# The first mixer kind in another order: two-softmax heads first, then the scan, plain attention last

## The reference, cut to what matters

```python
h = rms_norm(x, attn_norm[l])
proj = h @ w_in[l]                      # 1024 x 3072, padded to 26 chunks of 128 columns
a_q, a_k, a_v, b_q, b_k, b_v, c_q, c_ff, c_fb, c_v, c_g = split_columns(proj)
# A: plain attention, 6 query heads on 2 key heads of width 64, normed and rotated (rope)
aq = rope(rms_norm(a_q)); ak = rope(rms_norm(a_k)); o_a = softmax(aq ak^T / 8) @ av
# B: 4 heads, each the difference of two softmaxes of width 48, value width 96
p = softmax(q1 k1^T * s + bias) - lam * softmax(q2 k2^T * s + bias)
o_b = rms_norm(p @ bv) * (1 - lam_init)
# C: gated linear scan, both directions, 4 heads of 64
f = lb + (1 - lb) * sigmoid(c_ff or c_fb); cq = silu(c_q)
o_c = rms_norm(scan_forward + scan_backward) * silu(c_g)
x = x + concat(o_a, o_b, o_c) @ w_out[l]
```

## Time and profile before

| | us |
|---|---|
| Profiled execution, its own time | 1835.33 |
| Its span on the core | 1833.6 |
| TensorE busy | 1673.1 (91%) |
| VectorE busy | 1273.2 (69%) |
| ScalarE busy | 988.9 (54%) |
| GpSimd busy | 531.1 (29%) |
| TensorE clock granted, mean | 0.948 of full |
| First mixer of this kind, first unit to first output unit | 17.00 to 191.77 |
| Second mixer of this kind | 405.95 to 573.94 |

### The profile page before, as it was taken

The page is one execution under the profiler, slowest core; times in us unless marked ns, Lnnn a source line. Parts: engine busy times, 40 slices in busy tenths (PEclk is TensorE's granted clock), DMA queues, the critical chain, the costliest instruction groups (busy, mean ns, idle before and its releaser), DMA issues. The chain is left out here.

```text
span 1833.6 us, 30207 instructions
## 1 busy us (share of the span) xinstructions
PE 1673.1 (91%) x10188; PEld 1448.8 (79%) x10188; DVE 1273.2 (69%) x2018; ACT 988.9 (54%) x1530; POOL 531.1 (29%) x511
## 2 busy tenths in 40 slices
PE   5896899999976999999999476999999999799999
PEld 5785799888856999888888335888888888568888
DVE  5675677756776777667757877777577765757763
ACT  5455466545563666466644344665376535446652
POOL 3040433310312334134410003443144411434430
PEclk9998899999997999999999658999999999789999
DMA  6330355654311456555654202556555654225563
GB/s 229 104 116 24 100 181 185 219 169 139 104 58 57 163 185 204 184 177 188 209 186 133 86 1 86 178 185 215 164 181 185 209 180 149 69 92 184 186 217 102
DMA packets 70793, 274.12 MB, mean 150 GB/s; under 512 B 7872, under 2 KB 9024, under 8 KB 70592
## 3 DMA queue, kind: packets, MB, share of 16 engines
q1 hardware_dynamic: 70272, 271.04, 45.9%
q0 software_dynamic: 448, 2.13, 0.3%
HBM read 272.09 MB, written 1.05 MB: 149 GB/s over the span
## 5 line engine op out<-in xcount | busy, mean ns | idle before, releaser
L761 DVE TENSOR_TENSOR wl<-raw,wh 128x1024 fp32r<-128x1024 f32 (+1 forms) x474 | 626.6, 1322 | 104.7 <-ACT wh L507 98.1
L507 ACT ACTIVATE wh<-raw 128x1024 fp32r<-128x1024 f32 (+1 forms) x474 | 529.2, 1118 | 211.9 <-PE gb L1170 125.2
L1166 PE MATMUL gb<-hx,wh 128*128 128x512 f32 x1540 | 554.0, 399 | 0.0
L1167 PE MATMUL gb<-hx,wl 128*128 128x256 f32 x1540 | 432.3, 281 | 0.0
L1166 PE MATMUL gb<-gux,wh 128*128 128x512 f32 x960 | 341.1, 394 | 0.0
L1166 PEld LDWEIGHTS gb<-hx,wh 128*128 128x128 f32 x1540 | 289.8, 188 | 60.7
L1153 PE MATMUL gb<-hx,wh 128*128 128x256 f32 x1008 | 299.2, 297 | 24.8 <-DVE wl L761 17.4
L1167 PEld LDWEIGHTS gb<-hx,wl 128*128 128x128 f32 x1540 | 291.0, 189 | 7.9
L1154 PE MATMUL gb<-hx,wh 128*128 128x256 f32 x1008 | 288.7, 286 | 0.0
L1155 PE MATMUL gb<-hx,wl 128*128 128x256 f32 x1008 | 288.2, 286 | 0.0
L1167 PE MATMUL gb<-gux,wl 128*128 128x256 f32 x960 | 268.1, 279 | 0.0
(11 more groups left out here) (213 smaller groups left out, 2140.7 us busy)
## 6 DMA issues: line engine op xcount, KB each, us to landing
raw<-in_wa SPq DMA_DIRECT2D x378, 512.0 KB, 3.5
raw<-in_wb SPq DMA_DIRECT2D x96, 704.0 KB, 4.1
x<-in_x SPq DMA_DIRECT2D x1, 1024.0 KB, 5.0
out_x<-x SPq DMA_DIRECT2D x8, 128.0 KB, 3.2
row<-in_row POOLq DMA_DIRECT2D x1, 836.0 KB, 10.6
tab<-in_bias SPq DMA_DIRECT2D x3, 256.0 KB, 4.6
con<-in_const POOLq DMA_DIRECT2D x1, 544.0 KB, 7.7
tab<-in_bias SPq DMA_DIRECT2D x1, 512.0 KB, 5.2
```

What stands on the lines that cost most here:

```text
L507: nc.scalar.activation(wh[:, slot, 0:nt * P], raw[:, slot, 0:nt * P], ACT.Copy).then_inc(s_hi, 1)
L761: nc.vector.tensor_tensor(wl[:, slot, 0:nt * P], raw[:, slot, 0:nt * P], wh[:, slot, 0:nt * P].bitcast(f32), ALU.subtract).then_inc(s_lo, 1)
L1166: nc.tensor.matmul(bank[:, :], a, both(k), start=start and k == 0, stop=False)
L1167: nc.tensor.matmul(bank[:, 0:SEQ], b, high(k), start=False, stop=False)
```

## The change

Chunks, heads and steps of `mix1` get a new order; head steps are entries of their own (`turnp`, `score`, `prob`, `attend`) in place of `attn`, and `out_norms` is split into `stats` (statistics) and `post` (scaling and on). For `even` and `odd`, `spread` writes each old `attn` entry out as the four new ones in the order the engines had.

```diff
-M1_AQ, M1_AK, M1_AV, M1_CQ, M1_CF, M1_CB, M1_CG, M1_CV, M1_BV, M1_B = 0, 3, 4, 5, 7, 9, 11, 13, 15, 18
-A_ORDER = [0, 3, 1, 4, 2, 5]
+M1_CQ, M1_CF, M1_CB, M1_CG, M1_BV, M1_CV, M1_AK, M1_AV = 4, 6, 8, 10, 12, 19, 22, 25
+M1_AQ = (23, 24, 21)
+M1_B = (0, 2, 15, 17)
+A_ORDER = [2, 5, 0, 3, 1, 4]
...
-        W = {"mix1": [(1, "sqr", 0), (2, "sum", 0), (2, "norm", 0), (3, "sqr", 1), (4, "sum", 1), (4, "norm", 1),
-                      (5, "rotate", 0), (5, "rope", 0), (6, "turn", 0), (7, "rotate", 1), (7, "rope", 1),
-                      (9, "attn", 0), (10, "attn", 1), (11, "attn", 2), (12, "attn", 3), (13, "attn", 4), (13, "gates", 0),
-                      (14, "attn", 5), (16, "level", 0), (17, "turn", 1), (17, "level", 1), (18, "turn", 2),
-                      (18, "level", 2), (19, "level", 3), (19, "turn", 3), (20, "level", 4), (20, "turn", 4), (20, "sqr", 2),
-                      (21, "level", 5), (21, "sum", 2), (21, "norm", 2), (22, "level", 6), (22, "sqr", 3), (23, "level", 7),
-                      (23, "sum", 3), (23, "attn", 6), (23, "norm", 3), (24, "level", 8), (24, "sqr", 4), (25, "sum", 4),
-                      (25, "norm", 4), (25, "attn", 7), (25, "sqr", 5), (26, "cout", 0), (26, "sum", 5), (26, "norm", 5)] +
-                     [(26, "attn", t) for t in range(8, 14)] + [(26, "post", 0)],
+        W = {"mix1": [(1, "sqr", 0), (2, "sum", 0), (2, "norm", 0), (3, "sqr", 1), (4, "score", 0), (4, "sum", 1), (4, "norm", 1),
+                      (6, "prob", 0), (6, "score", 1), (7, "turnp", 0), (8, "prob", 1), (9, "turnp", 1), (12, "gates", 0),
+                      (13, "turn", 0), (14, "turn", 1), (15, "turn", 2), (15, "level", 0), (16, "attend", 0), (16, "level", 1),
+                      (17, "sqr", 2), (17, "attend", 1), (17, "level", 2), (18, "sum", 2), (18, "norm", 2), (18, "level", 3),
+                      (19, "sqr", 3), (19, "level", 4), (19, "score", 2), (20, "sum", 3), (20, "norm", 3), (20, "prob", 2),
+                      (20, "level", 5), (21, "turnp", 2), (21, "turn", 3), (21, "level", 6), (21, "score", 3),
+                      (22, "attend", 2), (22, "prob", 3), (22, "level", 7), (23, "sqr", 4), (23, "turnp", 3), (23, "level", 8),
+                      (23, "sum", 4), (23, "norm", 4), (24, "attend", 3), (24, "cout", 0), (25, "sqr", 5), (25, "rotate", 0),
+                      (25, "sum", 5), (25, "rope", 0), (25, "stats", 0), (25, "norm", 5), (26, "score", 4), (26, "turn", 4),
+                      (26, "rotate", 1), (26, "rope", 1), (26, "score", 5), (26, "prob", 4), (26, "turnp", 4), (26, "score", 6),
+                      (26, "prob", 5), (26, "post", 0), (26, "turnp", 5), (26, "score", 7), (26, "prob", 6), (26, "attend", 4),
+                      (26, "turnp", 6), (26, "score", 8), (26, "prob", 7), (26, "attend", 5), (26, "turnp", 7), (26, "score", 9),
+                      (26, "prob", 8), (26, "attend", 6), (26, "turnp", 8), (26, "prob", 9), (26, "attend", 7),
+                      (26, "turnp", 9), (26, "attend", 8), (26, "attend", 9)],
...
-            return u % 4 if kind != "mix1" or u < 13 else u % 2
+            return u % 4 if kind != "mix1" or u < 12 else u % 2
...
             def rope(m, g):
-                yv, tmp = pair(yc(2 * g, 2)), pair(ptb[:, 0, :])
+                yv, tmp = pair(yc(M1_AQ[2] + 2 * g, 2)), tap[:, :, :]
-                nc.vector.tensor_tensor(tmp, pair(MISC[:, :]), both(C_SIN), ALU.mult)
+                nc.vector.tensor_tensor(tmp, pair(gb[3][:, :]), both(C_SIN), ALU.mult)
...
-            def out_norms(m, l):
+            def out_stats(m, l):
                 dve.wait_ge(m["c_copied"], 1)
                 dve.wait_ge(m["attn_copied"], 4)
...
+            def out_norms(m, l):
+
                 dve.wait_ge(m["stats_rsd"], 1)
...
-                elif what == "post":
+                elif what == "stats":
                     act.wait_ge(m["stats"], 1)
...
             def scores(m, kind, l, hs, t):
-                if kind == "mix1":
-                    pe.wait_ge(m["roped"], 2)
+                if kind == "mix1" and need >= 4:
+                    pe.wait_ge(m["roped"], need - 3)
```

More of the change, by code:

```diff
@@ L271, in build_program, with spread @@
         NL = len(LEVELS)
-        W = {"mix1": [(1, "sqr", 0), (2, "sum", 0), (2, "norm", 0), (3, "sqr", 1), (4, "sum", 1), (4, "norm", 1),
-                      (5, "rotate", 0), (5, "rope", 0), (6, "turn", 0), (7, "rotate", 1), (7, "rope", 1),
-                      (9, "attn", 0), (10, "attn", 1), (11, "attn", 2), (12, "attn", 3), (13, "attn", 4), (13, "gates", 0),
-                      (14, "attn", 5), (16, "level", 0), (17, "turn", 1), (17, "level", 1), (18, "turn", 2),
-                      (18, "level", 2), (19, "level", 3), (19, "turn", 3), (20, "level", 4), (20, "turn", 4), (20, "sqr", 2),
-                      (21, "level", 5), (21, "sum", 2), (21, "norm", 2), (22, "level", 6), (22, "sqr", 3), (23, "level", 7),
-                      (23, "sum", 3), (23, "attn", 6), (23, "norm", 3), (24, "level", 8), (24, "sqr", 4), (25, "sum", 4),
-                      (25, "norm", 4), (25, "attn", 7), (25, "sqr", 5), (26, "cout", 0), (26, "sum", 5), (26, "norm", 5)] +
-                     [(26, "attn", t) for t in range(8, 14)] + [(26, "post", 0)],
+        def spread(steps, count):
+            for u, what, t in steps:
+                if what != "attn":
+                    yield u, what, t
+                    continue
+                for part, late in (("turnp", 3), ("score", 0), ("prob", 1), ("attend", 4)):
+                    if 0 <= t - late < count:
+                        yield u, part, t - late
@@ L296, in build_program @@
                      (16, "pool", 2), (16, "attn", 9), (16, "pool", 3), (16, "attn", 10), (16, "attn", 11)]}
+        W = {k: list(spread(W[k], len(heads(k)))) for k in W}
         def outputs(kind, what, t):
-            if what == "attn":
-                hs = heads(kind)
-                return 1 if 4 <= t < len(hs) + 4 and hs[t - 4].chunk is not None and t % 2 == 1 else 0
+            if what == "attend":
+                return 1 if heads(kind)[t].chunk is not None and t % 2 == 1 else 0
             return {"post": 3, "ln": 4, "pool": 1}.get(what, 0)
@@ L334, in group_of @@
         def group_of(kind, l, c):
-            return max(g for g, (c0, _, _) in enumerate(qk_groups(kind, l)) if c0 <= c)
+            return next(g for g, (c0, gains, _) in enumerate(qk_groups(kind, l)) if c0 <= c < c0 + len(gains))
         T0 = [16 * sum(is_mix[:n + 1]) for n in range(NPH)]
@@ L601, in do @@
                     nc.scalar.activation(tv[:, :, at0:at0 + w * P], pair(MISC[:, :])[:, :, 0:w * P], ACT.Copy).then_inc(m["v_tokens"], 1)
-                elif what == "attn":
-                    attention(m, kind, heads(kind), g)
+                elif what == "turnp":
+                    copy_turned(m, g)
+                elif what == "score":
+                    softmax_exp(m, heads(kind), g)
+                elif what == "attend":
+                    copy_attended(m, heads(kind), g)
                 elif what == "gates":
@@ L1021, in do @@
                     convolve(m, g // 4, g % 4)
-                elif what == "attn":
-                    attention(m, kind, heads(kind), g, l)
+                elif what == "score":
+                    row_max(m, heads(kind), g)
+                elif what == "prob":
+                    normalise(m, heads(kind), g, l)
+                elif what == "attend":
+                    low_attended(m, kind, heads(kind), g)
                 elif what == "level" and 1 <= g <= NL:
                     level(m, g)
+                elif what == "stats":
+                    out_stats(m, l)
                 elif what == "post":
@@ L1271, in attend @@
                 groups = V_GROUPS[kind]
-                pe.wait_ge(m["v_tokens"], 1 if kind == "mix1" and h.chunk is not None else len(groups))
+                pe.wait_ge(m["v_tokens"], 3 if h.chunk is None else len(groups))
                 pe.wait_ge(m["probsT"], t + 1)
@@ L1285, in attend @@
                     j = t // 2
-                    if j >= 1 and t % 2 == 0:
-                        pe.wait_ge(m["mix_lo"], before(kind, "attn", 2 * j + 3) + 1)
+                    if t and hs[t - 1].chunk is None:
+                        pe.wait_ge(m["attn_copied"], 4)
+                    elif j >= 1 and t % 2 == 0:
+                        pe.wait_ge(m["mix_lo"], before(kind, "attend", t - 1) + 1)
                     for kt in range(2):
@@ L1313, in do @@
                     last.then_inc(m["v_transposed"], 1)
-                elif what == "attn":
-                    hs = heads(kind)
-                    if 3 <= g < len(hs) + 3:
-                        turn_probs(m, hs, g - 3)
-                    if g < len(hs):
-                        scores(m, kind, l, hs, g)
-                    if 4 <= g < len(hs) + 4:
-                        attend(m, kind, hs, g - 4)
+                elif what == "turnp":
```

(5 more changed lines are left out.)

103 lines of the change are left out of this document (47 added, 56 removed).

## The result

| | before | after |
|---|---|---|
| Median of 4 runs each, us | 1840.38 (1834.74 to 1840.59) | 1863.04 (1860.0 to 1866.29) |
| Ratio (that of the two medians is 1.0123, inside the interval) | | 1.0135, 95% interval 1.0117 to 1.0153 |
| Profiled run, its span | 1835.33, 1833.6 | 1860.0, 1858.2 |
| Mean granted clock | 0.948 | 0.943 |

The change makes the kernel 22.7 us slower, by the medians; 1863 was forecast. I cut each mixer of this kind in two: the middle, from the first unit to the end of the last unit (25), and the end, from there to the first output unit.

What follows compares the result with a forecast made beforehand. Units were taken as TensorE-bound, the end as a chain of waits. Per mixer +19.9 us of stalls, -10.5 at the end and +4.2 for clock gave 27.6 for two; added to 1835.3 this made 1863, range 1838 to 1884.

Steps and rivals of the forecast that it cites:

- The middle: First unit to end of unit 25: new stalls sum to 26.8 us; chained, unit 25 ends 19.9 us later per mixer.
- score 1: Second B head's scores, after unit 6: TensorE waits 3.8 us, group 1's norm being behind the first head's exponentials.
- turnp 1: Turn of the second B head's probabilities, after unit 9: TensorE waits 3.2 us behind VectorE's evictions, splits and normalising.
- gates: Turn of gate chunks after unit 13: gates take 10.45 us, one unit covers 3.07, so TensorE waits 7.4 us.
- level 4: Scan level after unit 18: waits 3.2 us because group 2's norm stands ahead of level 3.
- turnp 2: Turn of the third B head's probabilities, units 19 to 21: waits 5.5 us behind exponentials, group 3's norm and normalising.
- turnp 3: Turn of the fourth B head's probabilities: waits 1.4 us, with prob 3 ahead of level 7.
- level 8: Late scan level: waits 1.5 us, with prob 3 ahead of level 7.
- turnp 0: Turn of the first B head's probabilities, before unit 9 ends: TensorE waits 0.8 us.
- The end: After unit 25, a chain mostly along VectorE: 38.2 us against 48.7, saving 10.5 us per mixer at full clock.
- The clock: TensorE's lower clock behind stalls: 1.7 us in the middle and 2.5 at the end, +4.2 us per mixer.
- cold: Rival: stalls throw TensorE to 1.2 GHz for the middle's stretches and the whole end; 1884 us, chance 0.18.

Runs made afterwards that it cites:

- e1: Kernel after, with the first gate-chunk transpose moved one unit later, behind unit 14: 1859.31 us, ratio 1.0117 to the kernel before.
- e2: Kernel after, with level 3 ahead of group 2's norm, and prob 2 and level 5 ahead of group 3's: 1856.93 us, ratio 1.0106.
- e6: Kernel after, with four banks up to unit 15 and the three gate and value turns behind unit 15: 1855.41 us, ratio 1.0116.
- e8: Kernel after, plus 129 small matmuls per mixer, each group shorter than its wait, in middle and end: 1846.55 us, ratio 1.0049.
- e10: Kernel before, plus small matmuls (9, 9 and 40 per mixer) in three waits at the end: 1829.54 us, ratio 0.9968.
- e4: Kernel after, plus 84 small matmuls in each mixer's end, which outlasted the waits: 1865.75 us, ratio 1.0156 to the kernel before.
- e11: e9 plus small matmuls (7, 8, 7, 9 and 17 per mixer) ahead of its five longest waits: 1804.28 us, ratio 0.9831.
- e9: Kernel after with a reworked list, four banks up to unit 15 and post's low halves as a separate step: 1818.12 us, ratio 0.9901.
- e3: Kernel after, with the branches' norm undivided again, statistics directly ahead of post: 1871.44 us, ratio 1.0181 to the kernel before.

## Why the prediction was right, step by step

**The middle.** Forecast +19.9 for stalls and 1.7 for the clock, 21.6; measured +22.1 and +22.7. In the second mixer this was 18.3 us more idle time and 4.3 more busy time of TensorE, close to the forecast's parts; in the first it was 14.0 idle and 8.1 busy, at a lower clock, so there the sum came out by a trade between the two that I had not worked out. The single waits, forecast and measured:

| | `score 1` | `turnp 1` | gates | `level 4` | `turnp 2` | `turnp 3` | `level 8` |
|---|---|---|---|---|---|---|---|
| forecast | 3.8 | 3.2 | 7.4 | 3.2 | 5.5 | 1.4 | 1.5 |
| measured, second mixer | 3.62 | 2.65 | 7.82 | 2.95 | 6.26 | 0.95 | 1.23 |
| measured, first mixer | 3.62 | 1.73 | 7.82 | 2.95 | 3.53 | 0.48 | 1.24 |

Only the forecast 0.8 at `turnp 0` has no row of its own. The chains could be worked out because every engine takes its part of each entry in the list's order, so one needs the durations and the list, no scheduler. e1, e2 and e6 show the causes of three of these waits: move the entry, and its wait goes or shrinks. That the time falls by as much they don't show.

**The end.** Forecast 38.2 at the full clock and 40.7 with it. e8's end, at a clock of 1.00, took 37.16 twice; the kernel after took 42.71 and 41.48. The order's own gain was right (e8 against e10, 37.16 against 47.4 and 46.5, is 9.8 on average; forecast 10.5), though e10's ends ran at 0.89 and not at the full clock. Two details missed: the wait of `post` is 5.77, not under 5, and the middles ended at 147.9 and 141.9, not about 139.

**The clock.** Forecast +4.2 per mixer, from two stretches of 7 us in the middle and a quarter of the end. Kernel after less e8, minus kernel before less e10, gives for the four stages +0.6, +4.0, +3.4 and +2.1: 10.1 in the mixers, where 8.4 was forecast, and 5.7 to 9.9 over whole launches. (1.5 of the +3.4 is that e10's second middle, 120.81 us, is longer than that of before, which is within the noise of a middle.) So the term had about its size as a difference. As a mechanism it was too simple in one respect: I asked where the new order idles and took the old order's clock as given, but the low stretches also move and vary between launches, and a slower TensorE waits less at the next step. That is the likely reason why e1, e2 and e6 gave 4 to 8 us by the medians, 3 to 5 by the ratios, where their waits promised more.

**The sum.** The mixers grew by 31.3 where 27.6 was forecast, and the span by 24.6, since about 4 us came back in the output units and 3 in an unchanged mixer. I had counted nothing outside. Over the launch the forecast was thus +27.6, measured +24.6 between the profiled executions and +22.7 between the medians. That 1863 is nonetheless the very median is luck: I started from an execution (1835.3) that lies 5.1 us below the median of before, and that made up for a change put 4.9 us too high. The mechanism doesn't hang on it: at the full clock I had +9.4 per mixer, 18.8, and e8 against e10 gives 17.0.

**The rule on the clock.** Ends of thin work ran at 0.67 to 0.75, and small matmuls alone brought them to 1.00 (e4, e8, e11). The Trainium skill (TensorE: Matmul & The Clock Gate, What's actually happening), weighed as the rival "cold", has the clock low unless activity releases it. The trace agrees in part: the ends were not wholly low, as the rival took it, and its 1884 is 21 us from the result.

## What to carry to other kernels

In a list that in-order engines share, look for each latency chain (here a group's norm, 3.84 us on ScalarE, and the gates, 10.45 us over two engines) and put between its start and its first reader as many independent units as it lasts; banks decide how many there can be. Put short steps that TensorE needs next (a scan level, a turn) ahead of long ones that nobody needs yet. What waits are left can be filled with small matmuls, sized below the wait from a measured one: that was worth 6 to 11 us in the kernel before, 16 in that after, and 13 to 14 in e9 (by the ratios and by the medians). Most of it came at the ends and in the output units behind them, little in the middles.

## What the runs showed of the hardware that I had not expected

- A wait can be paid twice, but not each is. Ahead of a 3.0 us stall and behind it the clock of before was 1.00; behind the 7.82 us stall of the kernel after a unit's matmuls started 0.21 us apart, not 0.12, for some 2.3 us (484.27 to 486.55). The length of the wait doesn't decide alone: the 4 us behind the 2.12 us wait at the first `turn` of before ran at 0.57 in the first mixer and at 1.00 in the second.
```profile
49.16:53.16 4.00, 4.00 (x21) 4.00 (x22) 1.32 (x2) 0.38 (x1) 0.00 (x0) 0.57 0.55 185
433.10:437.10 4.00, 4.00 (x29) 3.52 (x30) 1.75 (x3) 1.00 (x2) 0.00 (x0) 1.00 0.57 201
```
- One float32 matmul of 128x128 by 128x128 is two instructions and took 0.23 us of TensorE's time at the full clock: 30 of them fill 6.86 us ahead of the gates' wait, of which 1.12 us is left, in e8's timeline:
```profile
468.94 6.86 PE L1322 MATMUL gb<-con 128*128 128x128 f32 x60
476.92 0.33 PE L1346 MATMUL mb<-con,y 128*128 128x128 f32 x1 [1.12 <-DVE qq L867]
```
- The same middle, code and data, took 141.94 us in one launch and 145.30 in another (e3), at mean clocks of 0.94 and 0.88. Stage times of single profiles can't price an edit of 3 us; at the ends the fillers, which hold the clock at 1.00, made the two mixers of a launch agree (e8's 37.16 and 37.16, e11's 31.36 and 31.34, against 42.71 and 41.48 without).
